# VectorE's order in the attention, a shared key projected in two passes, and the last normed rows stored from ScalarE's queue

## The chip, the cores and the metric

The kernel runs on one core of a Trainium2 chip: TensorE (matmuls; PE in the profile, with PEld for its weight loads), VectorE (DVE), ScalarE (ACT), GpSimd (POOL), SyncE (SP, which here only issues transfers) and 16 DMA engines. The engines run their own queues of instructions and wait for each other by semaphores. The metric is the time of one execution in microseconds.

## The reference, cut to what matters

One decoder layer over 1,024 tokens and 16 learned meta tokens ahead of them, width 1,024, in float32.

```python
u = rmsnorm(h, attn_norm)
c_q, c_kv, k_pe, hq, hf, hi, hg, gm, gh = split(u @ w_in)   # k_pe: 32 columns, the rotary key that all heads share
o_mla = mla_branch(...)     # q, k, v from the latents c_q, c_kv; 8 heads, causal softmax(q k) v
o_hg = hgrn2_branch(...)    # a gated linear recurrence in chunks
h = h + (sigmoid(gm + b) * (o_mla @ w_br_mla) + sigmoid(gh + b) * (o_hg @ w_br_hgrn)) @ w_out
u = rmsnorm(h, ffn_norm)
h = h + hier_moe(u, ...)    # 64 experts: best group, then its best two; silu(x @ w1[e]) * (x @ w3[e]) @ w2[e]
out = rmsnorm(h, final_norm)[:, 16:]
```

## The kernel before

Everything is written by hand, each engine's queue in program order, with a semaphore for each kind of hand-over. There are three stages.

**Projection.** `project_part` runs a list of jobs, one for each 128 columns of `w_in`, in pieces of up to 512 stream positions. To keep float32's precision, weights and activations are split into a high and a low part (`wh`, `wl`; `uTh`, `uTl`), and `mm3` adds three products for each eighth of the contraction: high by high, high by low, low by high. Job `p`, the shared key, has only 32 columns. It comes behind the latents (`c`, `k`) and ahead of the gates (`s`), in three pieces of 352, 352 and 336 positions. ScalarE copies each piece to `kpe` (the tile `h_q`).

**Attention.** `attention_part` takes pairs of heads (n = 0 to 3) and blocks of query rows (i = 0 to 7), 32 steps k in all; block i sees 128 (i + 1) key columns. For each of the two heads of a step the chain is: TensorE's scores, VectorE's `peak` (adds the mask on the diagonal block, then takes the negated row maximum), ScalarE's exponential `expo` with the row sum, VectorE's `normed` (reciprocal of the sum, then the product), TensorE's `turn` (transposes of the block), copies to SBUF by ScalarE and VectorE, and TensorE's `weighted` product with the values. TensorE issues for step k: turn of the first head, scores of the next step's first head, turn of the second head, scores of the next step's second head, a piece of the branch projection (`fill`), `weighted`. VectorE's queue for a step is written out in `vector`. Step 7 (`BREAK`) holds the last 16 query rows besides.

**Output, routing and experts.** `merge_part` and `output_part` finish the layer's first half in blocks of 128 tokens (t = 0 to 7), store h and the normed rows u, and choose the experts. Of the last block ScalarE makes the normed rows. `experts_part` gathers u rows for two experts at a time (GpSimd, through a list of row numbers `src`) and multiplies them with the weights of 64 experts, which pass through seven buffers: `load_up` brings w1 and w3 of an expert, 1 MiB each, `load_down` brings w2, 1 MiB. SyncE issues all of these. The loads of the first seven experts are placed among the stores of `output_part`; from then on a buffer is loaded again when TensorE is through with it.

## Time and profile before

| | us |
|---|---|
| median of 3 runs | 1494.26 (1493.94 to 1495.15) |
| the profiled execution | 1496.1 |
| its span, first to last instruction | 1494.4 |
| TensorE busy | 1377.6 (92%) |
| VectorE busy | 581.8 (39%) |
| ScalarE busy | 561.4 (38%) |
| GpSimd busy | 101.6 (7%) |

The profile is of one execution. The projection lies at 0 to 577 us of the span, the attention at 577 to 786, merge, output and routing at 786 to 964, the experts at 964 to about 1436, the final norm behind that. Matmuls are pipelined and their ends are modelled: they start closer together than they are shown long, so a busy TensorE isn't one at its peak. A transfer's landing comes well after its issue. Idle time of an engine counts only where the others wait for it.

### The profile page before, as it was taken

The page shows a single profiled execution, that of the slowest core. Times are in us where ns is not written, and L with a number is a line of the kernel's source. Part 1 is how long each engine was busy: PE and PEld are TensorE (multiplying, and loading weights), DVE is VectorE, ACT ScalarE, POOL GpSimd, SP SyncE. Part 2 cuts the span into 40 slices and gives each one's busy share as a digit, 9 for nine tenths or more (in the row PEclk, how much of TensorE's full clock was granted, in tenths as well). Part 3 has the DMA queues.
Part 4 walks back from the last instruction along what each step waited for, and adds up shares of the span by engine and source line. Part 5 has one row for each costly group of instructions (what it writes and reads, how often), then busy time and mean ns, then how long its engine had stood idle before and what let it go on. Part 6 is the DMA issues. An engine that isn't in the chain of part 4 may idle for free. (4 is left out here: it accounts for less than half of the span.)

```text
span 1494.4 us, 21048 instructions
## 1 busy us (share of the span) xinstructions
PE 1377.6 (92%) x8471; PEld 983.6 (66%) x8471; DVE 581.8 (39%) x1303; ACT 561.4 (38%) x1066; POOL 101.6 (7%) x131
## 2 busy tenths in 40 slices
PE   5999999999999999999999999999987878688786
PEld 5888887787888887666667888855544444344442
DVE  6455565432531054656677556411110111111117
ACT  6534355222322146444552355533322222222223
POOL 0000000000000000000000011311111111111100
PEclk9999999999999999989999999999999999999998
DMA  6111111112234333112137654999999999999998
GB/s 185 43 29 43 29 29 43 30 32 78 80 97 122 101 89 124 57 36 71 36 120 240 253 194 157 321 416 415 415 416 416 416 417 416 416 416 417 415 403 333
DMA packets 130433, 312.53 MB, mean 209 GB/s; under 512 B 31120, under 2 KB 77200, under 8 KB 113184
## 3 DMA queue, kind: packets, MB, share of 16 engines
q1 hardware_dynamic: 118304, 285.96, 51.2%
q0 software_dynamic: 12032, 25.22, 4.4%
q8 instruction: 68, 1.11, 0.3%
q14 instruction: 29, 0.24, 0.0%
HBM read 283.81 MB, written 41.98 MB: 218 GB/s over the span
## 5 line engine op out<-in xcount | busy, mean ns | idle before, releaser
L2397 PE MATMUL ps<-r,m_xT 128*64 128x256 f32 x2048 | 253.4, 403 | 68.2 <-DMA r<-in_w 67.6
L130 PE MATMUL ps<-uTh,h_wh 128*128 128x512 f32 (+3 forms) x696 | 263.8, 379 | 4.4 <-DVE uTl L566 2.4
L131 PE MATMUL ps<-uTl,h_wh 128*128 128x512 f32 (+3 forms) x696 | 255.9, 368 | 0.0
L132 PE MATMUL ps<-uTh,h_wl 128*128 128x512 f32 (+3 forms) x696 | 255.6, 367 | 0.0
L2397 PEld LDWEIGHTS ps<-r,m_xT 128*64 128x64 f32 x2048 | 150.6, 145 | 153.5 <-DMA r<-in_w 76.1
L130 PEld LDWEIGHTS ps<-uTh,h_wh 128*128 128x128 f32 (+1 forms) x696 | 129.4, 186 | 28.7 <-DVE uTl L566 4.3
L2313 DVE TENSOR_TENSOR m_prod<-m_sig,ps 128x128 f32<-128x128 f32 x64 | 18.4, 288 | 333.4 <-ACT m_sig L2284 333.4
L132 PEld LDWEIGHTS ps<-uTh,h_wl 128*128 128x128 f32 (+1 forms) x696 | 129.3, 186 | 20.1
L131 PEld LDWEIGHTS ps<-uTl,h_wh 128*128 128x128 f32 (+1 forms) x696 | 129.6, 186 | 19.5 <-issue 0.2
L2379 PE MATMUL ps<-r,m_hT 128*64 128x512 f32 x512 | 122.4, 598 | 1.3 <-DVE m_hT L2317 0.9
L2274 ACT ACTIVATE m_y<-ps,gate 64x512 f32<-64x512 f32 x128 | 87.4, 682 | 80.0 <-PE ps L2379 78.4
L571 DVE TENSOR_TENSOR h_wl<-h_w,h_wh 128x1024 fp32r<-128x1024 f32 (+2 forms) x43 | 51.0, 1185 | 166.9 <-ACT h_wh L392 166.9
L2284 ACT ACTIVATE m_sig<-ps 128x128 f32<-128x128 f32 x64 | 17.8, 278 | 244.5 <-PE ps L2397 244.5
L1160 PE MATMUL ps<-KT,QT 96*128 96x512 f32 (+3 forms) x192 | 73.4, 494 | 0.0
L1131 ACT ACTIVATE t_p<-ps,t_negmax 112x128 f32<-112x128 f32 (+7 forms) x64 | 47.4, 741 | 63.7 <-DVE t_negmax L1233 63.6
L424 ACT ACTIVATE h_sg<-ps,h_bias 128x512 f32<-128x512 f32 x32 | 22.0, 688 | 131.2 <-PE ps L132 131.2
L627 DVE SCALAR_TENSOR_TENSOR h_S<-h_S,h_dec,ps 128x128 f32<-128x128 f32 x124 | 43.0, 347 | 55.9 <-PE ps L907 46.0
L2379 PEld LDWEIGHTS ps<-r,m_hT 128*64 128x64 f32 x512 | 34.1, 136 | 46.2 <-issue 38.1
L2317 DVE COPY m_hT<-ps 128x128 f32<-128x128 f32 x64 | 18.7, 292 | 102.6 <-PE ps L2408 102.6
L2226 POOL DMA_INDIRECT y_moe<-m_y,dst x31 | 30.9, 997 | 401.6 <-ACT m_y L2274 389.0
L455 ACT ACTIVATE h_kdn<-ps 128x128 f32<-128x128 f32 x32 | 8.9, 278 | 128.7 <-PE ps L886 128.7
L1328 PE MATMUL ps<-ident,t_p 128*128 128x128 f32 (+1 forms) x288 | 44.9, 283 | 8.3 <-DVE t_p L1241 8.3
(363 smaller groups left out, 2098.7 us busy)
## 6 DMA issues: line engine op xcount, KB each, us to landing
r<-in_w SPq DMA_DIRECT2D x190, 1024.0 KB, 24.3
h_w<-in_w_in SPq DMA_DIRECT2D x37, 512.0 KB, 4.3
gates<-h_sg POOLq DMA_DIRECT2D x16, 512.0 KB, 2.9
r<-y_moe SPq DMA_DIRECT2D x8, 1024.0 KB, 17.1
br_gate<-gates SPq DMA_DIRECT2D x14, 512.0 KB, 4.1
e_wo<-in_w_out SPq DMA_DIRECT2D x4, 1024.0 KB, 6.1
f_x<-in_x SPq DMA_DIRECT2D x8, 512.0 KB, 5.1
h_mid<-f_x SPq DMA_DIRECT2D x8, 512.0 KB, 4.5
```

Source lines behind the costliest of these rows:

```text
L130: pe.matmul(out, lh, rh, start=start, stop=False)
L131: pe.matmul(out, lh, rl, start=False, stop=False)
L132: return pe.matmul(out, ll, rh, start=False, stop=stop)
L571: dve.tensor_tensor(used(wl, J), used(w, J), used(wh, J).bitcast(F32), ALU.subtract).then_inc(wl_ok, 1)
L627: dve.scalar_tensor_tensor(out=S[:, (n + 1) % 8, :], in0=S[:, n % 8, :], scalar=dec[:, n:n + 1], in1=bank(KVB(ci), 0, P), op0=ALU.mult, op ...
L1131: act.activation(pr[b][0:rows(i), 0:P * (i + 1)], score(k, b, 0, P * (i + 1)), ACT.Exp, bias=negmax[0:rows(i), b:b + 1], accum_out=total[0 ...
L1160: ins = pe.matmul(score(k, b, c, w), g.QT[:, h, qcol(i):qcol(i) + rows(i)], g.KT[:, h, c:c + w], start=True, stop=True)
L1328: ins = pe.transpose(g.ps[:, (T_BANK + tbank(i, b, gi)) * 512 + x * P: (T_BANK + tbank(i, b, gi)) * 512 + x * P + rows(i)], pr[b][0:rows(i ...
L2226: pool.indirect_dma_start(out=g.y, out_offset=bass.IndirectOffsetOnAxis(ap=g.dst[:, n:n + 1], axis=0), in_=y[n % XB][:, :], in_offset=None ...
L2274: act.activation(y[i % XB][CAP * k:CAP * (k + 1), q * 512:(q + 1) * 512], bank(Y_BANK + e % 2, 0, 512, CAP * q, CAP * (q + 1)), ACT.Copy, ...
L2379: ins = pe.matmul(bank(Y_BANK + e % 2, 0, 512, CAP * f, CAP * (f + 1)), hT[:, j, :], g.r2[b][:, j, 512 * f:512 * (f + 1)], start=j == 0, s ...
L2397: ins = pe.matmul(bank(UP_BANK + e % 2, 0, DE, CAP * f, CAP * (f + 1)).rearrange("p (r f) -> p r f", r=2), xT[i % 2][:, j, CAP * k:CAP * ( ...
```

## The change

It has three parts.

1. The shared key. The low part of its weights is put beside the high part, in columns 32 to 63 of the same tile, and TensorE multiplies these 64 columns with the high and then the low activations: two matmuls in place of three for each eighth of the contraction, 48 in place of 72. Rows 0 to 31 of the result are then the high weights' products, rows 32 to 63 the low weights'. ScalarE copies the first as before, and VectorE adds the second to them (`summed_p`), a new instruction for each of the three pieces; TensorE takes the bank up again when that is done. The product of low weights and low activations, which the kernel before leaves out, is in the sum now.
2. VectorE's order in the attention. `peak` of the second head of the next step is taken ahead of `normed` of the first head; before, that was so in the last step only.
3. The end of `output_part`. The normed rows of the last block are stored by ScalarE, right behind the instruction that makes them, not by SyncE. On SyncE's queue the `load_down` of buffers 4 and 5 no longer stand behind that store, and the first MiB of buffer 6 goes ahead of the store of the last h rows, not behind the wait for the first gathered rows.

```diff
                 elif kind == "p":
                     if n == 0:
                         act.wait_ge(m_ok, 4 * HG)
-                    act.activation(kpe[0:ROPE, c:c + m], bank(p % 3, 0, m, ROPE), ACT.Copy).then_inc(p_ok, 1)
+                    act.activation(kpe[0:ROPE, c:c + m], bank(p % 3, 0, m, ROPE), ACT.Copy).then_inc(pp_ok, 1)
...
+            def summed_p(n):
+
+                c0, m = cols_of(LAT + 5)[n]
+                at_bank = spot[LAT + 5, n] % 3 * 512
+                dve.wait_ge(pp_ok, n + 1)
+                dve.tensor_tensor(kpe[0:ROPE, c0:c0 + m], kpe[0:ROPE, c0:c0 + m],
+                                  g.ps[ROPE:2 * ROPE, at_bank:at_bank + m], ALU.add).then_inc(p_ok, 1)
...
+                if JOBS[J][0] == "p":
+
+                    for j in range(4 * y, 4 * y + 4):
+                        for u_one in (g.uTh, g.uTl):
+                            last = pe.matmul(bank(p % 3, 0, m, 2 * ROPE), wh[J % 2][:, j, 0:2 * ROPE], u_one[:, j, col:col + m],
+                                             start=j == 0 and u_one is g.uTh, stop=j == DK - 1 and u_one is g.uTl)
...
-                if k + 2 == len(steps):
+                if more:
 
                     peak(k + 1, 1)
                     normed(k + 1, 0)
-                    normed(k + 1, 1)
-                elif more:
-                    normed(k + 1, 0)
-                    peak(k + 1, 1)
                     normed(k + 1, 1)
...
             sp.wait_ge(w_mm, 2 * TT)
-            store_u(TT - 1)
             g.load_down(sp, 4, 4)
             g.load_down(sp, 5, 5)
+            g.load_up(sp, 6, 6, (0,))
             store_h(TT - 1)
 
             sp.wait_ge(g.x_in[0], 16)
-            g.load_up(sp, 6, 6)
+            g.load_up(sp, 6, 6, (1,))
             g.load_down(sp, 6, 6)
...
                     act.activation(u[:, :], u[:, :], ACT.Copy, scale=sc[:, 14:15]).then_inc(u_ok, 1)
+                    act.wait_ge(u_ok, TT)
+                    act.dma_start(g.u2[t * P:(t + 1) * P, :], u[:, :]).then_inc(u_out, 16)
```

TensorE's queue where the shared key begins, before (the last two matmuls of the job ahead, then those of the key):

```order
L131 MATMUL ps<-uTl,h_wh 128x336
L132 MATMUL ps<-uTh,h_wl 128x336
L130 MATMUL ps<-uTh,h_wh 32x352 [waits h_raw_ok,h_wl_ok]
L131 MATMUL ps<-uTl,h_wh 32x352
L132 MATMUL ps<-uTh,h_wl 32x352
```

The same place of the changed kernel:

```order
L131 MATMUL ps<-uTl,h_wh 128x336
L132 MATMUL ps<-uTh,h_wl 128x336
L860 MATMUL ps<-uTh,h_wh 64x352 [waits h_raw_ok,h_wl_ok]
L860 MATMUL ps<-uTl,h_wh 64x352
L860 MATMUL ps<-uTh,h_wh 64x352
```

Each eighth of the contraction has two matmuls now, of 64 result rows, and the weights come from the tile `h_wh` alone.

VectorE's queue in the attention, before, in the step that prepares block i = 3 (512 columns) of a pair of heads. L1232 and L1233 are `peak`, L1239 and L1241 `normed`, L1247 the low part of a finished output; `t_s_mm0` and `t_s_mm1` are the scores of the first and the second head, `t_exp_ok0` and `t_exp_ok1` their exponentials:

```order
L1232 TENSOR_TENSOR ps<-ps,mask 128x128 [waits t_s_mm0]
L1233 TENSOR_REDUCE t_negmax<-ps 128x1 [waits t_dv]
L1247 TENSOR_TENSOR omTl<-ps,omTh 128x240 [waits t_oh_ok]
L1239 RECIPROCAL t_inv<-t_total 128x1 [waits t_exp_ok0]
L1241 TENSOR_SCALAR t_p<-t_p,t_inv 128x512 [waits t_dv]
L1232 TENSOR_TENSOR ps<-ps,mask 128x128 [waits t_s_mm1]
L1233 TENSOR_REDUCE t_negmax<-ps 128x1 [waits t_dv]
L1239 RECIPROCAL t_inv<-t_total 128x1 [waits t_exp_ok1]
L1241 TENSOR_SCALAR t_p<-t_p,t_inv 128x512 [waits t_dv]
```

The same step of the changed kernel, where these lines are L1250, L1251, L1257, L1259 and L1265:

```order
L1250 TENSOR_TENSOR ps<-ps,mask 128x128 [waits t_s_mm0]
L1251 TENSOR_REDUCE t_negmax<-ps 128x1 [waits t_dv]
L1265 TENSOR_TENSOR omTl<-ps,omTh 128x240 [waits t_oh_ok]
L1250 TENSOR_TENSOR ps<-ps,mask 128x128 [waits t_s_mm1]
L1251 TENSOR_REDUCE t_negmax<-ps 128x1 [waits t_dv]
L1257 RECIPROCAL t_inv<-t_total 128x1 [waits t_exp_ok0]
L1259 TENSOR_SCALAR t_p<-t_p,t_inv 128x512 [waits t_dv]
L1257 RECIPROCAL t_inv<-t_total 128x1 [waits t_exp_ok1]
L1259 TENSOR_SCALAR t_p<-t_p,t_inv 128x512 [waits t_dv]
```

Both reductions come ahead of both normalisations, and the wait for the second head's scores ahead of that for the first head's exponential.

SyncE's queue at the end of the output stage, before (`r13_4` is the w1 and w3 of buffer 4, `r2_4` its w2, `f_u` the normed rows, `f_x1` the h rows):

```order
L1469 DMA r13_5<-in_w3 128x2048
L1648 DMA u_moe<-f_u 128x1024
L1473 DMA r2_4<-in_w2 128x2x1024
L1473 DMA r2_5<-in_w2 128x2x1024
L1644 DMA h_mid<-f_x1 128x1024
L1469 DMA r13_6<-in_w1 128x2048
L1469 DMA r13_6<-in_w3 128x2048
L1473 DMA r2_6<-in_w2 128x2x1024
```

And in the changed kernel:

```order
L1483 DMA r13_5<-in_w3 128x2048
L1487 DMA r2_4<-in_w2 128x2x1024
L1487 DMA r2_5<-in_w2 128x2x1024
L1483 DMA r13_6<-in_w1 128x2048
L1658 DMA h_mid<-f_x1 128x1024
L1483 DMA r13_6<-in_w3 128x2048
L1487 DMA r2_6<-in_w2 128x2x1024
```

The u store is gone from this queue, and one load of buffer 6 stands ahead of the h store.

## Rows read from the trace of the kernel before

**Rows 1.** Busy time by stage: start:end, each engine, granted clock, DMA share, GB/s
```profile
core 0: us, PE busy (x) PEld busy (x) DVE busy (x) ACT busy (x) POOL busy (x), PEclk, DMA share, GB/s
577.00:786.00 209.00, 197.63 (x1451) 137.28 (x1449) 134.64 (x313) 101.34 (x244) 1.20 (x2) 0.98 0.19 66
786.00:949.00 163.00, 162.85 (x822) 137.03 (x823) 101.23 (x303) 75.99 (x154) 17.86 (x25) 0.99 0.64 225
...
1069.00:1436.00 367.00, 300.36 (x2030) 159.72 (x2028) 39.98 (x138) 98.98 (x181) 46.29 (x46) 0.95 1.02 416
```

**Rows 2.** The chain of waits, at the experts: start, us, what
```profile
1072.58 25.87 DMA r<-in_w
```

**Rows 3.** Timeline of TensorE around the shared key: start, us, engine, line, operation
```profile
333.68 0.32 PE L131 MATMUL ps<-uTl,h_wh 128*128 128x336 f32 x1
333.83 0.31 PE L132 MATMUL ps<-uTh,h_wl 128*128 128x336 f32 x1
...
333.98 0.32 PE L130 MATMUL ps<-uTh,h_wh 128*32 128x352 f32 x1
...
345.33 0.40 PE L130 MATMUL ps<-uTh,h_wh 128*128 128x512 f32 x1
```

**Rows 4.** TensorE's waits, 577 to 778 us: us in total, times, longest
```profile
PE ps L1328 <- DVE t_p L1241: 7.1, 10, 1.1
```

**Rows 5.** Timeline of a step with 512 key columns
```profile
699.50 1.02 PE L1160 MATMUL ps<-KT,QT 96*128 96x512 f32 x2
...
701.12 0.40 DVE L1247 TENSOR_TENSOR omTl<-ps,omTh 128x240 fp32r<-128x240 f32 x1
...
702.05 0.16 DVE L1239 RECIPROCAL t_inv<-t_total 128x1 f32<-128x1 f32 x1 [0.53 <-ACT t_p L1131]
...
702.65 0.29 DVE L1232 TENSOR_TENSOR ps<-ps,mask 128x128 f32<-128x128 f32 x1
...
702.79 0.66 PE L1328 MATMUL ps<-ident,t_p 128*128 128x128 f32 x4
702.97 0.69 DVE L1233 TENSOR_REDUCE t_negmax<-ps 128x1 f32<-128x512 f32 x1
...
703.70 0.69 ACT L1131 ACTIVATE t_p<-ps,t_negmax 128x512 f32<-128x512 f32 x1 [1.68 <-DVE t_negmax L1233]
...
704.71 0.49 DVE L1241 TENSOR_SCALAR t_p<-t_p,t_inv 128x512 f32<-128x512 f32 x1
...
705.25 0.66 PE L1328 MATMUL ps<-ident,t_p 128*128 128x128 f32 x4 [0.73 <-DVE t_p L1241]
```

**Rows 6.** Timeline of the next step, 640 key columns
```profile
705.74 1.25 PE L1160 MATMUL ps<-KT,QT 96*128 96x512 f32 x4
...
707.54 0.56 DVE L1241 TENSOR_SCALAR t_p<-t_p,t_inv 128x640 f32<-128x640 f32 x1
...
708.34 0.82 DVE L1233 TENSOR_REDUCE t_negmax<-ps 128x1 f32<-128x640 f32 x1
...
709.34 0.76 PE L1328 MATMUL ps<-ident,t_p 128*128 128x128 f32 x5
```

**Rows 7.** Timeline of SyncE's transfers at the end of the output stage
```profile
937.59 2.20 SPq L1469 DMA_DIRECT2D r<-in_w  x4
950.33 0.33 SPq L1648 DMA_DIRECT2D u_moe<-f_u  x1
950.70 1.39 SPq L1473 DMA_DIRECT2D r<-in_w  x2
...
963.87 0.81 SPq L1469 DMA_DIRECT2D r<-in_w  x2
```

**Rows 8.** Granted clock, DMA share and GB/s of a stretch there
```profile
950.00:952.00 2.00, 1.00 0.52 197
```

**Rows 9.** The chain of waits there
```profile
955.68 0.20 DVE src L1968
...
956.77 7.08 DMA rows<-u_moe,src
```

**Rows 10.** Landing of the u store issued at 950.33
```profile
DMA to landing us min/median/max: 4.5/4.5/4.5
```

More of the change, by code:

```diff
@@ L211, in project_part @@
         sg_out = [sem(f"h_sg_out{b}") for b in range(2)]
+        pp_ok = sem("h_pp_ok")
         raw_ok, p_ok, ns_ok, ms_mm, nr_ok, n_ok, nh_ok, nl_ok = (
@@ L570, in low @@
                 dve.wait_ge(wh_ok, J + 1)
-                dve.tensor_tensor(used(wl, J), used(w, J), used(wh, J).bitcast(F32), ALU.subtract).then_inc(wl_ok, 1)
+                low_part = wh[J % 2][:, :, ROPE:2 * ROPE] if JOBS[J][0] == "p" else used(wl, J)
+                dve.tensor_tensor(low_part, used(w, J), used(wh, J).bitcast(F32), ALU.subtract).then_inc(wl_ok, 1)
             def forget(r):
@@ L779, in vector @@
                         low_o(HG - 1, s // 2 - 10)
+                    if B == HG and s in (27, 29):
+                        summed_p(s // 2 - 13)
+            summed_p(2)
             for n in range(NB):
@@ L840, in half @@
                 col, m = cols_of(J)[n]
-                rows = ROPE if JOBS[J][0] == "p" else P
                 if cols_of(J) is REAL:
                     col += META
-                for j in range(4 * y, 4 * y + 4):
-                    last = mm3(pe, bank(p % 3, 0, m, rows), wh[J % 2][:, j, 0:rows], wl[J % 2][:, j, 0:rows], g.uTh[:, j, col:col + m],
+                if JOBS[J][0] == "p":
[3 more added lines that the diff above has]
+                                             start=j == 0 and u_one is g.uTh, stop=j == DK - 1 and u_one is g.uTl)
+                for j in range(4 * y, 4 * y + 4) if JOBS[J][0] != "p" else ():
+                    last = mm3(pe, bank(p % 3, 0, m), wh[J % 2][:, j, :], wl[J % 2][:, j, :], g.uTh[:, j, col:col + m],
                                g.uTl[:, j, col:col + m], j == 0, j == DK - 1)
@@ L1465, in expert_loaders, with load_up @@
     down = g.w2[0].rearrange("e (j p) n -> p e j n", j=2)
-    def load_up(eng, e, b):
-        for r in range(2):
+    def load_up(eng, e, b, parts=(0, 1)):
+        for r in parts:
             eng.dma_start(g.r13[b][:, r, :, :], up[r][:, bass.ds(e, 1), :, :].rearrange("p a j f -> p (a j) f")
```

## The prediction

> **What bounds the kernel now.** I read the stages first [rows 1]. TensorE is busy 197.63 of 209 us in the attention (577 to 786) and 162.85 of 163 us in the merge and output stage behind it; from 1069 to 1436 it is busy 300.36 of 367 us, while the DMA engines are at a share of 1.02 and 416 GB/s. So there are two limits, one after the other: TensorE up to about 950 us and the stream of expert weights up to about 1436 us. The chain of waits says the same of the second part: TensorE is followed back to 1069, and behind it stand weight transfers, one of 25.87 us from issue to landing [rows 2]. Two things follow. Time taken from TensorE before 950 us moves everything behind it forward, the weight stream too, since its loads wait for events of TensorE; it is worth its full amount. And in the expert stage only bytes that are moved earlier, into time in which the DMA engines idle, are worth anything.
>
> The profiled execution took 1496.1 us around a span of 1494.4 us; the median of the runs is 1494.26 us, 1.84 us less. I sum against 1496.1 and take 1.84 off at the end.
>
> **Part 1, the shared key on TensorE.** The 72 narrow matmuls start at 333.98, and the first matmul of the next job starts at 345.33 [rows 3]: 11.35 us, 0.158 us each, back to back. The changed kernel issues 48, of the same moving widths (352, 352, 336 columns). Only the stationary side is wider, 64 columns in place of 32. The job ahead has 128 stationary columns and starts its last two matmuls of 336 columns at 333.68 and 333.83, 0.15 apart [rows 3], so the stationary width doesn't set the pace. 24 x 0.158 = **3.8 us** less; lower bound 3.0, if every one of the 48 were 0.015 longer, the rounding of two rows. What is added: VectorE sums two row halves three times, 32 rows by 352. TensorE takes each of these banks up again only after two other pieces, at least 32 matmuls or 5 us, and VectorE has nothing else in its queue there, so a sum of some 0.5 us (the subtraction of 240 columns in [rows 5] takes 0.40) is covered. With that cover gone it would be three times that, 1.5 us. The store of the low part into the other weight tile moves no work.
>
> **Part 2, VectorE's order in the attention.** In this stage, without its last step, whose order is left as it was, TensorE waits ten times for VectorE's normalisation of a block of probabilities, 7.1 us in all, 1.1 at most [rows 4].
>
> One step shows why they arise [rows 5]. VectorE is done with the low part of the output at 701.12 + 0.40 = 701.52. It then idles 0.53 us for the exponential of the first head (reciprocal at 702.05), normalises, and only then takes the second head's maximum, which ends at 702.97 + 0.69 = 703.66. ScalarE starts the second exponential at 703.70, VectorE normalises at 704.71, and TensorE, which had been waiting 0.73 us, turns the second head's block at 705.25. With the maximum first, it starts at about 701.5 instead of 702.65, since its scores were done at 699.50 + 1.02 = 700.5, and ends at 702.5. The second exponential starts 1.2 us earlier, and the second normalisation, now 703.3 plus the queue behind the first, ends near 704.0. TensorE then turns it when its scores are issued, with no wait. The price is on the first head: its normalisation starts at 702.4 in place of 702.05, 0.3 to 0.4 us later, and here TensorE took it up at 702.79, at once. So this step gives back 0.3 us of 0.73 at worst, unless the earlier second head of the step before has moved VectorE forward too, which it has, for VectorE works behind the same chain.
>
> The wider steps have room for it [rows 6]. The scores end at 705.74 + 1.25 = 706.99, the first normalisation ends at 707.54 + 0.56 = 708.10, and TensorE comes for it at 709.34. With the maximum (0.29 + 0.82, 1.15 us with the link) in front, from 707.0 to 708.2, the normalisation ends at 708.85, still 0.5 us ahead of TensorE. The new wait on the second head's scores stands ahead of the first head's normalisation, and behind it in VectorE's queue are both normalisations and whatever gate product or weight split follows; TensorE waits for the first of them.
>
> The waits are counted from modelled ends. Matmuls that start 0.158 apart are shown 0.32 long [rows 3], so each wait may be 0.16 us longer in starts: 7.1 + 1.6 = 8.7 is the upper bound. Taking off 0.3 for four steps of the kind in [rows 5] gives 7.5, and I take **7.5 us**. The lower bound is nothing, if each wait only changes heads.
>
> **Part 3, the last normed rows and the weights.** Up to now SyncE issues 4 MiB of weights at 937.59, is then held by the last u rows until 950.33, stores them, and issues 2 MiB more at 950.70; the 3 MiB of buffer 6 wait for the first gathered rows and go at 963.87 [rows 7]. The DMA engines are half idle at 950 to 952, a share of 0.52 [rows 8]. In the changed kernel SyncE isn't held: the 2 MiB go when TensorE's last output product ends, and then the first MiB of buffer 6, all before the last rows are normed. One MiB is 2.52 us at 416 GB/s. It leaves the saturated stream, and it fits into the idle stretch only in part: 0.96 us of 950 to 952 are filled at once, the rest pushes against the gather of the first rows, which takes 7.08 us [rows 9] and shares the engines. The bounds are 3.5 us (1 MiB and the 0.96) and, at the other end, a loss, below. I take **2.0 us**. The store instruction itself moves to ScalarE and costs there what it cost SyncE, 0.33 us [rows 7], ahead of the gate shares; VectorE's selection runs on meanwhile, so I put it at nothing, 0.33 if exposed.
>
> What the gather waits for matters here. The store was issued at 950.33 and took 4.5 us to land [rows 10], 954.8; VectorE's list of rows was done at 955.68 + 0.20 = 955.9 [rows 9]. So the store has 1.05 us to spare, and an earlier landing gains nothing. On a queue of its own it no longer stands behind the weights of buffers 4 and 5, but shares the engines with 3.5 MiB behind them. At half the rate its 0.5 MiB take 2.5 us in place of 1.26, which puts it at 956.1, 0.2 us late. If it had to let all of it pass, 3.67 MB or 8.8 us, it would land at 963.6, the gather would start 7.8 us late, and the gain of 2.5 would become a loss of 5.3.
> The Trainium skill speaks against this part: "DMA: Bandwidth & Descriptors", section "Issuing engines are not separate DMA queues", says that transfers of different issuing engines run on the same 16 DMA engines and interleave, so a second issuing engine saves only the issue time. By it the move alone would be worth at most the 0.33 us of the issue, and the part would be worth only what the earlier weights bring. No run here shows two hardware queues side by side.
>
> **Sum.** 3.8 + 7.5 + 2.0 = 13.3 us. 1496.1 - 13.3 = 1482.8 for a profiled execution, and less 1.84 it is **1481.0 us** for the median.
>
> **Rivals.**
> *The waits only change heads.* The first head's turn then waits for what the second's no longer does. For it speaks the step of [rows 5], where TensorE took the first head up at once; against it the 0.5 us left in [rows 6] and the wider steps. Part 2 gives 0 to 3: 1485.5 to 1488.5, near 1487.
> *Slower: the second head's scores block VectorE.* If TensorE, freed of its waits, reaches the first head in every step before the delayed normalisation, each of the 31 steps exposes the delay, 0.3 us in [rows 5] and 0.75 in [rows 6], say 0.65 on the mean: 20.1 us in place of a gain of 7.5, and with the 5.8 of the other parts 1494.26 + 14.3 = 1508.6. It ends slower from a mean exposed delay of 5.8/31 = 0.19 us on, if all ten old waits come back as well, or 0.43 if they stay gone. Against it: TensorE can't outrun VectorE here, as the scores that VectorE waits for are TensorE's own, issued ahead of a branch product and a weighted sum that stand before the turn.
> *The store lands late.* Shared engines delay the gather, and the earlier MiB buys nothing or costs: part 3 from 0 to 5.3 lost, 1483 to 1488.
> *The key part doesn't do what it says,* if the 64-column form runs at a slower pace: 1484.8. Nothing in the trace speaks for it.
>
> **Chances.** The forecast, each part near its size (1478 to 1484): 0.72. Waits change heads: 0.10. Store late: 0.10. Key slower: 0.02. Slower through VectorE: 0.03. More than 1478 allows, if short waits that the trace calls issue vanish too: 0.03. Leaving out the slow rival and the far ends of the others gives a range of 1476 to 1488. 0.2% is 3.0 us, about what a measurement of this kernel can tell from no change; all cases but the slow one end more than that below 1494.26, and I leave 0.03 for two of them coming together as no change: faster 0.94, same 0.03, slower 0.03.
>
> **What would show it.** Shared key: 48 matmuls in 7.6 us. Attention: TensorE's waits for the normalisation down from 7.1 to about 1 us, the stage shorter by 7 to 8. If instead turns of the first head show waits, part 2 was wrong. In the hand-over: SyncE issuing 3 MiB in one go ahead of the last u store, that store landing less than 5.5 us after its issue, and the gather still released by the row list; the experts' first DMA wait later than 1069 less the shift. A store that lands 7 us or more after its issue makes part 3 wrong. Since parts 1 and 2 lie in a TensorE that is otherwise full, a result above 1488 would mean that some wait of the attention has come back elsewhere.

## The result, and the profile of the changed kernel

The changed kernel took 1482.14 us (median of 4, 1480.37 to 1483.24) beside 1494.66 for the kernel before: a ratio of 0.9915, 95% interval 0.9898 to 0.9933. The forecast was 1481.0, between 1476 and 1488. The total is as forecast; two of its three terms are not, and they cancel. The order of VectorE gave more than 7.5 us, and the hand-over to the experts, forecast at 2.0 us gained, cost about 2: that the total fits is luck.

The stages of the profiled execution (1483.24 us, span 1481.5), the view of [rows 1], cut where the stages now lie:

```profile
core 0: us, PE busy (x) PEld busy (x) DVE busy (x) ACT busy (x) POOL busy (x), PEclk, DMA share, GB/s
0.00:575.00 575.00, 556.34 (x3127) 460.75 (x3128) 255.40 (x429) 224.79 (x379) 12.16 (x34) 1.00 0.26 72
575.00:772.00 197.00, 192.75 (x1447) 136.41 (x1446) 134.60 (x310) 104.85 (x240) 1.20 (x2) 0.98 0.21 70
772.00:935.00 163.00, 161.78 (x818) 135.16 (x819) 100.73 (x300) 75.34 (x153) 17.90 (x25) 1.00 0.63 223
935.00:951.00 16.00, 13.20 (x114) 12.87 (x113) 6.94 (x42) 6.63 (x14) 4.98 (x5) 1.00 0.99 342
951.00:1055.00 104.00, 103.50 (x752) 57.26 (x752) 13.87 (x48) 36.06 (x65) 18.16 (x18) 0.98 1.00 399
1055.00:1422.00 367.00, 309.86 (x2041) 164.36 (x2037) 39.58 (x137) 99.08 (x182) 46.30 (x46) 0.93 1.02 416
```

The attention went from 209 to 197 us. The stretch of 16 us ahead of the experts, 935 to 951, has a DMA share of 0.99 and 342 GB/s, where the like stretch of before, 949 to 965, had 0.83 and 278, so the idle DMA time of [rows 8] is filled, as intended. But of the 13.7 us by which the merge starts earlier (its first matmul stood at 786.10 and now stands at 772.41), only 12.8 reach the end of the span (1494.38 to 1481.54).

TensorE's waits from 570 to 775, the view of [rows 4]: the 7.1 us in ten waits for the normalisation are gone, and what is left are the two of the last step.

```profile
PE ps L1342 <- DVE t_p L1259: 1.2, 2, 0.8
PE ps L1360 <- ACT t_PT L1197: 0.3, 1, 0.3
```

The shared key on TensorE and VectorE's sums beside it, as in [rows 3]: 334.92 to 342.49 is 7.57 us in place of 11.35, and the sums of 0.5 us each lie under the matmuls.

```profile
334.92 0.32 PE L860 MATMUL ps<-uTh,h_wh 128*64 128x352 f32 x1
335.07 0.32 PE L860 MATMUL ps<-uTl,h_wh 128*64 128x352 f32 x1
...
342.49 0.40 PE L130 MATMUL ps<-uTh,h_wh 128*128 128x512 f32 x1
```
```profile
338.16 0.51 DVE L718 TENSOR_TENSOR h_q<-h_q,ps 32x352 f32<-32x352 f32 x1 [0.39 <-ACT h_q L421]
340.71 0.51 DVE L718 TENSOR_TENSOR h_q<-h_q,ps 32x352 f32<-32x352 f32 x1 [2.04 <-ACT h_q L421]
343.15 0.50 DVE L718 TENSOR_TENSOR h_q<-h_q,ps 32x336 f32<-32x336 f32 x1 [1.93 <-ACT h_q L421]
```

SyncE's transfers at the hand-over, the view of [rows 7]. The 3 MiB (three loads of 1 MiB: x2 and x1) go in one piece at 932.0 to 933.4, and the rest of buffer 6 at 951.36:

```profile
924.09 3.53 SPq L1483 DMA_DIRECT2D r<-in_w  x4
932.01 0.89 SPq L1487 DMA_DIRECT2D r<-in_w  x2
932.95 0.47 SPq L1483 DMA_DIRECT2D r<-in_w  x1
933.46 0.43 SPq L1658 DMA_DIRECT2D h_mid<-f_x  x1
951.36 0.33 SPq L1483 DMA_DIRECT2D r<-in_w  x1
951.73 0.44 SPq L1487 DMA_DIRECT2D r<-in_w  x1
957.88 0.80 SPq L1483 DMA_DIRECT2D r<-in_w  x2
```

And the chain of waits there, which [rows 9, 10] answer to:

```profile
935.62 1.16 ACT f_u L1829
936.79 9.47 DMA u_moe<-f_u
...
947.26 4.08 DMA rows<-u_moe,src
951.34 0.14 issue
951.48 1.57 PE ps L2382 x8
953.05 4.79 PE ps L2413 x32
```

This is where the forecast failed. The last u store was issued at 936.79, 13.54 us earlier than before, in step with everything ahead of it. It took 9.47 us to land, where it took 4.5. Before, the gather began 6.44 us after that issue (950.33 to 956.77), released by VectorE's list; now it begins 10.47 us after it, released by the landing. It is then shorter, 4.08 us in place of 7.08, since less stands ahead of it on the DMA engines. Net, the experts' first transposes come 14.69 us after the store's issue and not 13.66. Right behind stands something that the prediction didn't have: the first expert's 32 matmuls take 4.79 us in place of some 3.6 (3.67 in the timeline of before), at half clock.

```profile
949.00:952.00 3.00, 0.83 (x7) 0.67 (x7) 0.00 (x0) 0.00 (x0) 2.39 (x3) 1.00 0.69 208
952.00:955.40 3.40, 3.40 (x18) 2.12 (x18) 0.00 (x0) 2.48 (x3) 1.21 (x2) 0.50 0.86 258
```

TensorE was busy 0.83 of the 3 us from 949 on, and the granted clock was 0.50 (1.2 GHz) in the 3.4 us that followed. TensorE's waits for weights in the expert stage are 56.9 us (31 times) in place of 66.0 (32 times), yet the stage isn't shorter: from the first transposes to the end of the span it is 530.1 us in place of 530.4. TensorE stands less and works longer, 309.86 of 367 us in place of 300.36, at a granted clock of 0.93 in place of 0.95. That view measures how long TensorE stands, not how fast the weights come.

### The profile page after: what moved, and what is told of

It reads as the page before. It is cut to its first block and busy times, and to the rows that moved or that the text cites. A ratio compares the mean times of both kernels' runs of the same rounds, so it can differ in the third digit from the quotient of the medians.

```text
span 1481.5 us, 21002 instructions
## 1 busy us (share of the span) xinstructions
PE 1379.5 (93%) x8447; PEld 985.8 (67%) x8447; DVE 583.9 (39%) x1306; ACT 565.5 (38%) x1066; POOL 101.7 (7%) x131
## 5 line engine op out<-in xcount | busy, mean ns | idle before, releaser
L2413 PE MATMUL ps<-r,m_xT 128*64 128x256 f32 x2048 | 262.4, 414 | 59.4 <-DMA r<-in_w 59.2
L130 PE MATMUL ps<-uTh,h_wh 128*128 128x512 f32 (+2 forms) x672 | 256.3, 381 | 4.3 <-DVE uTl L567 2.4
L2413 PEld LDWEIGHTS ps<-r,m_xT 128*64 128x64 f32 x2048 | 154.4, 149 | 150.1 <-DMA r<-in_w 67.5
L131 PE MATMUL ps<-uTl,h_wh 128*128 128x512 f32 (+2 forms) x672 | 248.3, 370 | 0.0
L132 PE MATMUL ps<-uTh,h_wl 128*128 128x512 f32 (+2 forms) x672 | 248.1, 369 | 0.0
L2329 DVE TENSOR_TENSOR m_prod<-m_sig,ps 128x128 f32<-128x128 f32 x64 | 18.5, 288 | 335.0 <-ACT m_sig L2300 287.7
L130 PEld LDWEIGHTS ps<-uTh,h_wh 128*128 128x128 f32 x672 | 126.9, 189 | 27.4 <-DVE uTl L567 4.3
L132 PEld LDWEIGHTS ps<-uTh,h_wl 128*128 128x128 f32 x672 | 126.8, 189 | 18.9
L131 PEld LDWEIGHTS ps<-uTl,h_wh 128*128 128x128 f32 x672 | 127.2, 189 | 18.2 <-issue 0.2
L573 DVE TENSOR_TENSOR h_wl<-h_w,h_wh 128x1024 fp32r<-128x1024 f32 (+1 forms) x42 | 50.5, 1203 | 156.0 <-ACT h_wh L393 156.0
L1197 ACT ACTIVATE t_PT<-ps 128x512 f32<-128x512 f32 (+3 forms) x80 | 38.2, 498 | 50.5 <-PE ps L1342 50.0
```

The costliest lines, as they stand in the source:

```text
L130: pe.matmul(out, lh, rh, start=start, stop=False)
L131: pe.matmul(out, lh, rl, start=False, stop=False)
L132: return pe.matmul(out, ll, rh, start=False, stop=stop)
L573: dve.tensor_tensor(low_part, used(w, J), used(wh, J).bitcast(F32), ALU.subtract).then_inc(wl_ok, 1)
L2413: ins = pe.matmul(bank(UP_BANK + e % 2, 0, DE, CAP * f, CAP * (f + 1)).rearrange("p (r f) -> p r f", r=2), xT[i % 2][:, j, CAP * k:CAP * ( ...
```

## The experiments

Each kernel was timed in turn with the kernel before on one chip. The three groups of experiments come from different chips, on which the kernel before took 1493.99, 1494.54 and 1494.81 us. "Two parts" below is the kernel with the first two parts of the change and the hand-over as before. "Store to end" is the time from the issue of the last u store to the end of the span. It leaves out all that happens ahead of the hand-over, which differs from one execution to the next. It comes from the one execution of each kernel that was profiled.

### The order alone, and the key alone

```diff
 # the kernel before
-                if k + 2 == len(steps):
-                    peak(k + 1, 1)
-                    normed(k + 1, 0)
-                    normed(k + 1, 1)
-                elif more:
-                    normed(k + 1, 0)
-                    peak(k + 1, 1)
-                    normed(k + 1, 1)
+                if more:
+                    peak(k + 1, 1)
+                    normed(k + 1, 0)
+                    normed(k + 1, 1)
```

> The kernel before with VectorE's order alone. Theory A (the order is worth more than the 7.1 us of waits shown in the trace, since short waits that stand as issue or as stretched matmuls vanish too, and the attention was 10.9 us shorter): 9 to 10 us less, 1484.5 to 1485.5, first fill to merge 197 to 199 us in place of 208.1. Theory B (the order is worth 7.5 as forecast, and the other 3.4 us were time at half clock that fell differently in one execution): 1486.8, and a stage of 200.6 us at the same share of half clock. Theory C (the waits change heads): 1491 or more.

Measured: 1482.34 us, ratio 0.9929 (0.9915 to 0.9942), 11.65 us less than the 1493.99 of before in these rounds, and below what any of the three theories named. The same step as in [rows 5], with the first head's scores left out (those at 691.57 are the second head's):

```profile
691.57 1.02 PE L1160 MATMUL ps<-KT,QT 96*128 96x512 f32 x2
...
693.29 0.69 DVE L1233 TENSOR_REDUCE t_negmax<-ps 128x1 f32<-128x512 f32 x1
...
694.09 0.49 DVE L1241 TENSOR_SCALAR t_p<-t_p,t_inv 128x512 f32<-128x512 f32 x1
...
694.72 0.66 PE L1324 MATMUL ps<-ident,t_p 128*128 128x128 f32 x4
...
695.03 0.49 DVE L1241 TENSOR_SCALAR t_p<-t_p,t_inv 128x512 f32<-128x512 f32 x1
...
696.30 0.60 PE L1324 MATMUL ps<-ident,t_p 128*128 128x128 f32 x4
```

The first head is turned 3.15 us after these scores (3.29 before), the second 4.73 us after them (5.75 before). So the first head lost nothing, and the second gained 1.02 us where the trace of before showed a wait of 0.73. TensorE executes the same instructions in the same order in both kernels, so the two traces can be laid side by side, start by start. Outside the stretches at half clock the kernel with the new order is 9.5 us shorter, and 8.2 of it are the ten turns of a second head, each 0.5 to 1.0 us sooner; the rest are smaller gaps. Eight of the ten gained 0.16 us more than the wait that the trace of before shows for them; the two longest (1.12 us shown) gained 1.0. Inside the stretches at half clock it gained some 4 us more, because it had fewer of them: one of 3.4 us, where before had 10.2 us in the attention and 3.4 at the start of the merge. The granted clock from 620 to 660 of the kernel before, of the changed one and of this one shows them: 0.87, 0.91 and 0.96.

```profile
620.00:660.00 40.00, 38.62 (x359) 27.23 (x354) 19.11 (x51) 15.49 (x40) 0.00 (x0) 0.87 0.19 67
```
```profile
620.00:660.00 40.00, 39.68 (x378) 29.90 (x371) 23.88 (x62) 18.24 (x46) 0.00 (x0) 0.91 0.17 54
```
```profile
620.00:660.00 40.00, 39.67 (x384) 28.20 (x385) 22.84 (x59) 17.93 (x46) 0.00 (x0) 0.96 0.20 67
```

That is 10.2, 6.8 and 3.4 us at half clock. They fall differently in executions of like kernels: the attention, from the start of the first scores to that of the last turn's last matmul, took 196.6 us in the changed kernel at 0.91 and 195.1 in the one with two parts at 0.96, which is the same program up to there. Over all the kernels with the new order it took 193.5, 195.1, 196.6 or 198.1 us, with none, one, two or three stretches of 3.4 us in it. One such stretch therefore cost 1.5 us. Theory A holds for the 9.5. Part of the 11.65 is then clock, as B said, but on top of 9.5 and not of 7.5; how much of it in the median isn't shown, since only one execution was profiled.

```diff
 # the kernel before, with the first part of the change alone; its core:
+                    for j in range(4 * y, 4 * y + 4):
+                        for u_one in (g.uTh, g.uTl):
+                            last = pe.matmul(bank(p % 3, 0, m, 2 * ROPE), wh[J % 2][:, j, 0:2 * ROPE], u_one[:, j, col:col + m],
+                                             start=j == 0 and u_one is g.uTh, stop=j == DK - 1 and u_one is g.uTl)
```

> The kernel before with the shared key's two passes alone. Theory A (24 matmuls of 0.158 us less and everything else covered): 3.8 us less than before, 1490.2, and the 48 matmuls in 7.6 us. Theory B (the difference of 4.2 between the kernel with two parts and the one with the order alone holds something more, such as fewer stretches at half clock): 1489.5 or less.

Measured: 1489.12 us, ratio 0.9968 (0.9956 to 0.9980), 5.4 less than the 1494.54 of its rounds. The 48 matmuls run from 333.84 to 341.41, 7.57 us, so 3.8 us are the part itself. The remainder fits B: its granted clock from 620 to 660 is 0.91, two stretches where the trace of before has three. TensorE's waits for the normalisation, 570 to 781, stand at 8.3 us and 12 times, what the kernel before shows with its last step. They belong to the order alone:

```profile
PE ps L1346 <- DVE t_p L1259: 8.3, 12, 1.1
```

### Two parts: the hand-over as before

```diff
 # the changed kernel
             sp.wait_ge(w_mm, 2 * TT)
+            store_u(TT - 1)
             g.load_down(sp, 4, 4)
             g.load_down(sp, 5, 5)
-            g.load_up(sp, 6, 6, (0,))
             store_h(TT - 1)
             sp.wait_ge(g.x_in[0], 16)
-            g.load_up(sp, 6, 6, (1,))
+            g.load_up(sp, 6, 6)
...
-                    act.wait_ge(u_ok, TT)
-                    act.dma_start(g.u2[t * P:(t + 1) * P, :], u[:, :]).then_inc(u_out, 16)
```

> The shared key's two passes and VectorE's order, with the store and the weights of the hand-over as before. Theory A (the hand-over part gained nothing: its store landed 9.5 us after its issue, the gather started 4.0 us later against the rest of the program and gave 3.0 back by being shorter, and the first expert ran 3.4 us at half clock behind the longer idle time): store lands 4 to 5 us after issue, the gather is released by VectorE's list of rows and takes about 7 us, the experts' first transposes stand 13.5 us ahead of the kernel before instead of 12.5, time 1481 to 1482, no worse than the changed kernel's 1482.1. Theory B (the hand-over part is worth the 2.0 us forecast and the other two gave 10.5): 1484.1.

Measured: 1478.1 us (1477.43 to 1478.81), ratio 0.9894 (0.9879 to 0.9909). The median is 4 us below the changed kernel's and below what both theories named: the hand-over part didn't only gain nothing, it cost. But the intervals of the two ratios overlap, so both were run once more:

> The kernel with the first two parts again, for this call's chip. Theory A: 1478 (ratio 0.9894), 542.5 us from the last u store's issue to the end.

Measured: 1478.8 us, ratio 0.9903 (0.9884 to 0.9922), store to end 543.2 us, 542.5 the first time.

> The changed kernel once more, beside the kernels of this call, since 1482.1 against 1478.1 came from different chips. Theory A (the hand-over part costs 2 us from the last u store to the end, and the rest of the 4.0 is half clock that falls more often): 1481 to 1483, store landing 9 to 10.5 us after its issue, a stretch at half clock at the first expert's matmuls. Theory B (it was the chip): 1478 to 1479.5.

Measured: 1480.66 us, ratio 0.9911 (0.9898 to 0.9925), the store landing 9.2 us after its issue. Its trace and the first one with two parts are nearly equal up to the store, which was issued at 933.54 in the changed kernel and at 933.35 in the one with two parts, with the same 0.96 of clock from 620 to 660. The spans end at 1478.5 and 1475.8. Store to end is 544.9 against 542.5 us, 2.5 us for the third part. In the first comparison the two profiled spans were 5.7 us apart (1481.5 and 1475.8); 2.3 of it lie behind the store, 1.5 are one more stretch at half clock in the attention, and the rest lies in the projection (0.9) and in the merge and output stage (1.0), where the second trace of the changed kernel shows nothing of the kind. Over all traces the old hand-over stands at 544.1 (before), 543.3 (order alone), 542.6 (key alone), 542.5 and 543.2 (two parts), the new one at 544.8 and 544.9: 1.7 us between the means, with a scatter of 1.6 in the old one. The times of all executions say the same: nine of the changed kernel took 1480.17 to 1483.24 us; of eight with two parts seven took 1477.43 to 1479.37 and one 1482.84; the two medians are 2.4 us apart. I put the cost at 1.7 to 2.5 us. Theory A holds.

The store's landing in the kernel with two parts, the changed one (again), the one with the store moved alone and the one with one MiB ahead:

```profile
DMA to landing us min/median/max: 4.5/4.5/4.5
```
```profile
DMA to landing us min/median/max: 9.2/9.2/9.2
```
```profile
DMA to landing us min/median/max: 6.7/6.7/6.7
```
```profile
DMA to landing us min/median/max: 5.8/5.8/5.8
```

### Is it the queue or what stands ahead?

```diff
 # the changed kernel, store back on SyncE
             g.load_down(sp, 4, 4)
             g.load_down(sp, 5, 5)
             g.load_up(sp, 6, 6, (0,))
+            store_u(TT - 1)
             store_h(TT - 1)
```

> The changed kernel with the last u store back on SyncE, behind the 3 MiB of weights, so that only the queue of the store differs. Theory A (what delays the store is the 3 MiB ahead of it on the same DMA engines, whichever queue): it lands at about 945.7 to 947 (9 to 10 us after its issue), the gather is released by the landing, the time is that of the changed kernel, 1481.5 to 1483. Theory B (the second queue is what is slow: its packets are passed over by SyncE's): on SyncE's queue it lands clearly earlier, 941 to 943, and the time is 1480 to 1481.

Measured: 1481.45 us, ratio 0.9921 (0.9908 to 0.9935). The store landed 10.8 us after its issue and the gather began 11.8 us after it. So with the same 3 MiB of weights ahead the store is late on SyncE's queue too, even 1.3 to 1.6 us later than on ScalarE's, although the h store stands behind it here and ahead of it in the changed kernel. B is out as the reason for the late landing. Store to end is 546.5 us, the second longest of all.

```diff
 # the changed kernel, store on ScalarE, weights as in the kernel before
             sp.wait_ge(w_mm, 2 * TT)
+            sp.wait_ge(u_ok, TT)
             g.load_down(sp, 4, 4)
             g.load_down(sp, 5, 5)
-            g.load_up(sp, 6, 6, (0,))
             store_h(TT - 1)
             sp.wait_ge(g.x_in[0], 16)
-            g.load_up(sp, 6, 6, (1,))
+            g.load_up(sp, 6, 6)
```

> The changed kernel with the store on ScalarE's queue, but with all weights behind it as in the kernel before (2 MiB once the last u rows are normed, buffer 6 behind the gather). Theory A (the queue costs nothing, the weights ahead do): store lands 4 to 5 us after its issue, gather released by the list of rows, and from the store to the end 542.5 us, as with two parts, 1478. Theory B (a store on the second queue gives way to SyncE's loads even when it is issued with them): it lands 6.5 us or later after its issue, and 1 to 2.5 us are lost.

Measured: 1477.96 us, ratio 0.9895 (0.9878 to 0.9911), store to end 543.1 us. That time agrees with A (542.5 and 543.2 with two parts). The landing agrees with B: 6.7 us instead of 4.5, and the gather was released by it, 7.66 us after the issue. The gather was 0.5 us shorter for that (6.4 against 6.9 to the first transposes), and nothing beyond 0.3 us was lost. So a place on the second queue, beside 2 MiB issued at the same moment, costs this store 2.2 us against a place ahead of them on SyncE's queue. The packets show why the second queue is no way past the 3 MiB. In the changed kernel (again, store issued at 933.54) up to 937 all packets are SyncE's, of q1. The 144 packets of q10, ScalarE's, lie between 937 and 942, among 227 of q1:

```profile
q1 hardware_dynamic: 363, 1.42, 100.8%
```
```profile
q1 hardware_dynamic: 227, 1.00, 68.0%
q10 hardware_dynamic: 144, 0.52, 37.0%
```

The columns are packets, MB and share of the 16 engines. The store didn't start for 3.5 us and then got 0.52 MB through in 5, beside 1.0 MB of q1. While it ran in full it did have half: from 937.54 to 939.54 q10 moved 0.37 MB and q1 0.36. The prediction's 2.5 us, half the rate from the start on, took no account of the wait before the first packet, nor of the slow end: the last packet is through at 941.8, 4.8 us after the first began, and the landing is reported 0.9 us later. The store did overtake something. The h store, issued on SyncE's queue 3.3 us ahead of it, landed at 947.4, 4.7 us behind it:

```profile
h_mid<-f_x SPq DMA_DIRECT2D x1, 512.0 KB, 17.2
```

(The last figure is the us from issue, at 930.24, to landing.) The rule of the Trainium skill that the prediction drew on ("DMA: Bandwidth & Descriptors", "Issuing engines are not separate DMA queues") agrees: the two queues interleaved, and the move by itself gained nothing.

### How many MiB ahead?

```diff
 # two parts
             sp.wait_ge(w_mm, 2 * TT)
-            store_u(TT - 1)
             g.load_down(sp, 4, 4)
+            store_u(TT - 1)
             g.load_down(sp, 5, 5)
```

> The kernel with two parts, with one MiB of weights (the w2 of buffer 4) ahead of the last u store on SyncE in place of behind it. Theory A (the store stands behind what is ahead of it, but only a landing later than 6.0 us after the issue holds the gather up): it lands 6 to 7 us after its issue, the gather starts 0 to 1 us later and is shorter by as much, 542.5 to 543.5 us from store to end, 1478 to 1479, so the harm begins between one and three MiB. Theory B (each MiB ahead costs a third of the 2.5 us): 543.3 us.

Measured: 1478.66 us, ratio 0.9897 (0.9881 to 0.9912), store to end 541.6 us, 0.9 and 1.7 less than the two executions of two parts. The store landed after 5.8 us, in time: the gather was still released by the list, and TensorE didn't idle ahead of the transposes. It stood 1.4 us behind them instead, and the first expert's matmuls began 14.8 us after the store, as with two parts. So one MiB ahead is free or a little better, three are too much; two weren't tried. That is A's reading, except that it put the landing at 6 us or more and the end at 542.5 or later.

```diff
 # the changed kernel, store back on SyncE, ahead of the weights
             sp.wait_ge(w_mm, 2 * TT)
+            store_u(TT - 1)
             g.load_down(sp, 4, 4)
             g.load_down(sp, 5, 5)
             g.load_up(sp, 6, 6, (0,))
```

> The changed kernel with the last u store on SyncE as before, ahead of the weights, and the first MiB of buffer 6 kept ahead of the h store. Theory A: the store lands 4 to 5 us after its issue, the gather is released by the list of rows, takes 7 to 8.5 us among 3 MiB of weights, and the MiB that fills the idle stretch behind is worth 0 to 2.5 us over the kernel with the first two parts alone: 1479 to 1482. Theory B (the earlier MiB only slows the gather, by as much as it saves, since the stream must later wait for buffers that TensorE frees): equal to that kernel within 0.5 us.

Measured: 1481.95 us (1478.12 to 1484.14), ratio 0.9912 (0.9898 to 0.9925). The store landed in 4.6 us and the gather began 6.45 us after the issue, as with two parts, but the transposes came 8.2 us later in place of 6.9. Now the gather, not the store, stands behind the third MiB. The first expert ran at half clock here too. Store to end is 544.1, 0.9 and 1.7 above the two executions of two parts. A had the MiB as a gain and B at nothing; by this one trace it costs about 1.3 us, which is within the 1.6 by which traces with the old hand-over differ.

### Less ahead of the gather

```diff
 # two parts
             g.load_down(sp, 4, 4)
             g.load_down(sp, 5, 5)
-            store_h(TT - 1)
             sp.wait_ge(g.x_in[0], 16)
+            store_h(TT - 1)
             g.load_up(sp, 6, 6)
```

> The kernel with the first two parts (store and weights as before, 1478.1), with the last h store moved from ahead of the gather to behind its landing. Theory A (the gather's packets stand behind what SyncE has issued, 3.1 MB of it, and move up by as much as is taken from there, but 0.5 MB are then added to the full stream of weights behind): the gather takes 1 to 1.5 us less, TensorE idles less than 0.5 us ahead of the experts, and the time is the same within 1 us. Theory B (what counts is when the first expert starts, not the bytes in the stream): 1 to 1.5 us less, 1476.8.

Measured: 1479.78 us, ratio 0.9910 (0.9896 to 0.9923), store to end 544.8. The experts started 1.0 us sooner, as both theories said, and it ended 2.4 us later, which neither had. Behind the first three experts TensorE waits 3.5 us for a later gather (`PE ps L2380 <- DMA rows<-u_moe,src: 3.5, 1, 3.5`). GpSimd's queue shows its cause:

```profile
944.93 0.99 POOL L2216 DMA_INDIRECT y_moe<-rows,dst  x1 [0.30 <-issue]
955.46 1.04 POOL L2229 DMA_INDIRECT rows<-u_moe,src  x1 [9.54 <-DMA y_moe<-rows,dst]
```

With two parts the second line has 2.77 in its brackets. The scatter that zeroes rows of y is issued at 944.93 here, just behind SyncE's h store (944.26) and the first of its 3 MiB (944.64); with two parts it is issued 1.5 us ahead of them (945.06 and 946.54).

```diff
 # the same, with w2 of buffer 5 behind the gather too
             g.load_down(sp, 4, 4)
-            g.load_down(sp, 5, 5)
             sp.wait_ge(g.x_in[0], 16)
+            g.load_down(sp, 5, 5)
             store_h(TT - 1)
```

> The same, with the second MiB of weights (the w2 of buffer 5) behind the gather's landing too. Theory A: the gather takes 4.2 us, TensorE doesn't idle ahead of the experts, but 1.5 MB (3.8 us at 416 GB/s) are added to the stream, which starts 2.5 us earlier: 1 to 1.5 us slower than with two parts, 1479.3. Theory B: 1 us faster, 1477.

Measured: 1483.85 us, ratio 0.9925 (0.9911 to 0.9938), store to end 546.6, the same wait at 4.1 us. Both theories missed this by 4.5 us or more. To see whether the scatter or the bytes do it, SyncE then also waited for the scatter's landing, with the h store last:

```diff
 # the kernel of the h store behind
             sp.wait_ge(g.x_in[0], 16)
-            store_h(TT - 1)
+            sp.wait_ge(g.y_zero, 16)
             g.load_up(sp, 6, 6)
             g.load_down(sp, 6, 6)
+            store_h(TT - 1)
```

> The kernel of the h store behind, with SyncE's 3 MiB and that store held until GpSimd's scatter that zeroes rows of y has landed. Theory A (what spoiled it was this scatter, behind 3.5 MB of SyncE's, which held GpSimd for 9.5 us and so the gather for the third pair of blocks, for which TensorE waited 3.5 us): GpSimd waits 3 us or less, the third gather is issued before 16 us after the store, no wait of TensorE, and 541.5 to 543 us from the store to the end in place of 544.8. Theory B (the 0.5 MB in the full stream were the cause): 544 or more.

Measured: 1481.16 us, ratio 0.9917 (0.9901 to 0.9934), store to end 545.6. TensorE's wait is gone and GpSimd waits 2.7 us, as A said. The time is B's, though not its 0.5 MB alone: the 3 MiB are also issued 1.4 us later behind the store than with two parts (14.6 in place of 13.2), and this kernel doesn't part the two. TensorE has no stall for gathered rows any more, and still it takes 2.4 to 3.1 us more from store to end than two parts: DMA time that idles here is missed at the end.

The last view puts most of this in one number: the busy time of the 40 us behind the last u store, with share and GB/s at the end. In this order: one MiB ahead, two parts, the changed kernel again, h store behind, after the scatter.

```profile
934.28:974.28 40.00, 37.52 (x302) 26.89 (x302) 8.98 (x45) 14.61 (x28) 10.50 (x11) 1.00 0.96 372
```
```profile
933.35:973.35 40.00, 37.72 (x301) 26.95 (x302) 8.96 (x44) 14.56 (x28) 10.41 (x11) 1.00 0.94 362
```
```profile
933.54:973.54 40.00, 36.43 (x278) 26.37 (x277) 8.69 (x44) 13.37 (x26) 10.46 (x11) 0.96 0.95 337
```
```profile
933.22:973.22 40.00, 35.07 (x263) 25.12 (x263) 8.10 (x41) 12.91 (x25) 9.09 (x10) 0.91 0.90 337
```
```profile
938.22:978.22 40.00, 37.72 (x303) 27.02 (x304) 8.97 (x44) 14.55 (x28) 10.41 (x11) 1.00 0.88 327
```

372, 362, 337, 337 and 327 GB/s are 14.9, 14.5, 13.5, 13.5 and 13.1 MB in 40 us; store to end is 541.6, 542.5, 544.9, 544.8 and 545.6. Between the first and the last that is 2.2 us for each missing MB, and one MB takes 2.4 us at the stream's 416 GB/s. In the 15 us ahead of the store all fourteen traces moved 5.1 to 5.4 MB, so what is missing in the 40 us is really behind. The other nine are 365, 361, 359 and 357 GB/s at 543.3, 542.6, 543.2 and 543.1 us (order alone, key alone, two parts again, store moved alone), 355 at 544.1 (before), 343 at 544.8 (changed), 341 at 544.1 (store first), 332 at 546.6 (w2 of buffer 5 behind too) and 331 at 546.5 (store behind on SyncE). A straight line through all fourteen has 2.4 us for each MB; single traces lie up to 0.9 us off it. TensorE's column doesn't order them: the last kernel has as much TensorE work done in these 40 us as the second, and is 3.1 us slower.

This is also where the early MiB of the changed kernel went. It is 0.7 MB ahead of two parts 15 us behind the store, by the packets, and 0.95 MB behind it from 40 us on; from 40 to 200 us behind the store both move the same 415 GB/s, so the loss is made in these 40 us. The rest of buffer 6 is issued when the gather has landed, 14.5 us behind the store in place of 13.2, and TensorE frees the first buffer late: its matmuls begin 1.3 us later and take 1.7 longer at half clock, so that the next load goes at 21.5 us in place of 18.5. In between the DMA engines have little to do: from 947 to 949 they moved 114 GB/s and from 949 to 951 246. With two parts there is such a gap too, 108 GB/s from 945 to 947, but the stream is back at 393 from 949 on. How much of the loss is the late store and how much the half clock isn't shown.

## Why the prediction came out, step by step

**What bounds the kernel**: right. The time that TensorE lost or saved ahead of the hand-over reached the end, and behind it only the bytes counted.

**Part 1**, 3.8 us: right, 3.78 us between the same two matmuls, the sums covered.

**Part 2**, 7.5 us: the mechanism was right, the size wrong. The failed step is "Taking off 0.3 for four steps of the kind in [rows 5]" from the 8.7: nothing came off. The ten turns gained 8.2 us, and with 1.3 us of smaller gaps, which the sum hadn't, it was 9.5. No first head gave anything back; VectorE had moved forward, as the same paragraph had allowed. The 0.16 us per wait that modelled ends hide were real for eight of the ten. Fewer stretches at half clock came on top, 1.5 us each, which the prediction didn't have.

**Part 3**, 2.0 us gained: wrong in sign, 1.7 to 2.5 us lost. The failed step is "At half the rate its 0.5 MiB take 2.5 us in place of 1.26, which puts it at 956.1, 0.2 us late". The half rate came only after 3.5 us without a packet, and had a slow end. The store landed 9.2 to 9.5 us after its issue, beyond the 7 us named as the mark against this part. That is the rival *The store lands late*. The measured landing lies about half way between the forecast's (956.1, 5.8 us after the issue) and that rival's worst case (963.6, 13.3 us after it). Its price was smaller than the 5.3 us given there, since a later gather is a shorter one: of 4.0 us later 3.0 came back. And the gain that was set against it, 1 MiB earlier, wasn't there: the stream waited for the first expert's buffer afterwards, and with the store in time (landed after 4.6 us) the early MiB still brought nothing.

**The slower rival** (the second head's scores block VectorE) and **the waits only change heads**: no wait of a first head appeared, neither had any part in it.

**The sum**: 3.8 + 7.5 + 2.0 = 13.3 forecast. By the traces it is 3.8 + 9.5 - 2.1 = 11.2, the last term the middle of 1.7 to 2.5. The medians give 12.5 and, in the second timing, 13.9; the 1.3 to 2.7 us between are of the size of one or two stretches at half clock less, which the medians themselves can't show. The forecast of the total was right by luck, because a part that was too small and one of the wrong sign, with some clock on top, met near 13.

Left open: why the stretches at half clock in the attention come not at all in one execution and three times in another, and why the shared key begins at 333.4 in one trace and at 334.9 in another (334.92 in the changed kernel, 333.98 before), ahead of any change. Two parts with one MiB ahead of the store has the shortest time from store to end; by the whole time (1478.66) it can't be told from two parts alone (1478.1 and 1478.8) or from the store moved alone (1477.96).

## What to carry to other kernels

Where a wide transfer stream follows a small transfer on which the next stage waits, ask what stands ahead of the small one on the DMA engines at its issue; another queue gets past only part of it (9.2 to 9.5 us in place of 10.8, where 4.5 were possible). Fill idle DMA time with so much only as still lets the small one land in time (here one MiB did, three didn't, two weren't tried), and count an earlier load as a gain only if the loads behind it can move up too: their buffers must come free earlier. Compare such variants from the event at which they part to the end, not by the total, as long as the part ahead differs by more than the effect.

## What the runs showed of the hardware that was not expected

- A store on a second hardware queue, behind 3 MiB of the first: no packet for 3.5 us, then 0.52 MB in under 5 us beside 1.0 MB of the first queue; it landed after 9.2 to 9.5 us, and after 10.8 on the first queue itself. It landed 4.7 us ahead of a 0.5 MiB store that the first queue had been given 3.3 us earlier. Issued with nothing new ahead of it but together with 2 MiB it landed after 6.7 us, and after 4.5 when it stood ahead of them on their own queue.
- GpSimd's indirect transfers stand behind SyncE's as well: the gather took 4.1 us with little ahead of it and 7.1 behind the two MiB and the h store; the small scatter took 2.9 us issued ahead of SyncE's loads and 9.7 issued just behind them.
- TensorE waited 2.1 and 2.2 us for the gathered rows in the two executions of the changed kernel, 2.2 with the store first and 2.7 with the store behind on SyncE; in all four a granted clock of 0.50 followed at the first expert (3.4 us). It waited 0.8 and 1.2 us with two parts, 1.2 in the kernel before and 1.5 with the store moved alone, and the clock stayed at 1.00. The waits of 3.5 and 4.1 us for a later gather came with 6.8 us at 0.50. The 32 matmuls of the first expert cost 1.2 to 1.7 us more at half clock, which then holds up the buffer they free.
